# Feature-major matmuls of a two-layer transformer kernel: high weight tiles against 512 joined token columns, low tiles in a second pass

## What is computed

```python
def swiglu(x, w_gate, w_up, w_down):            # first network, two per layer
    return (jax.nn.silu(x @ w_gate) * (x @ w_up)) @ w_down      # 1024 -> 2816 -> 1024
...
z = u @ w_in[l]                                 # one wide projection per mixer
c_q, c_kv, k_rope, dq, dk, dv, p_in, z_gate = jnp.split(z, split_idx, axis=-1)
...
jnp.square(jax.nn.relu(x @ w1)) @ w2            # second network's feed-forward, 1024 -> 4096 -> 1024
```

## Time and profile before

| what | value |
|---|---|
| median of three executions | 2109.79 us (2108.17 to 2111.42) |
| profiled execution, its own time | 2109.59 us |
| span in the profile, first to last instruction | 2107.8 us |
| mean granted TensorE clock | 0.998 of full speed |
| TensorE matmul busy | 2079.7 us |
| VectorE busy | 1260.8 us |
| ScalarE busy | 1038.2 us |
| moved by DMA | 375.44 MB, mean 178 GB/s |

### The profile page before, as it was taken

One profiled execution on the slowest core, in us unless ns is written; L12 is line 12 of the kernel. 1 busy time (PEld: TensorE's weight loads), 2 busy tenths in 40 slices (PEclk: granted clock), 3 DMA queues, 4 the chain that ended last, 5 costly groups with the idle time before them and its releaser, 6 DMA issues.

```text
span 2107.8 us, 29081 instructions
## 1 busy us (share of the span) xinstructions
PE 2079.7 (99%) x12472; PEld 1843.5 (87%) x12472; DVE 1260.8 (60%) x1399; ACT 1038.2 (49%) x1327; POOL 89.7 (4%) x123
## 2 busy tenths in 40 slices
PE   7999999999999999999999999999999999999998
PEld 6999978889989898888898989888899888888897
DVE  5455586664455455676654565656755666567555
ACT  5444476454344344675443356643544466444442
POOL 1000100000000001000000000010100000100000
PEclk9999999999999999999999999999999999999999
DMA  8555444465566555444565564544755545455562
GB/s 297 181 190 181 156 159 140 140 210 181 189 193 211 182 185 191 147 143 140 169 218 183 176 221 134 176 152 153 243 183 193 192 154 180 150 175 196 188 192 80
DMA packets 178193, 375.44 MB, mean 178 GB/s; under 512 B 8480, under 2 KB 18848, under 8 KB 178064
## 3 DMA queue, kind: packets, MB, share of 16 engines
q1 hardware_dynamic: 174256, 360.67, 51.6%
q0 software_dynamic: 3808, 12.90, 2.0%
HBM read 372.49 MB, written 1.05 MB: 177 GB/s over the span
## 4 chain that ended last, share of the span: by engine, by line
PE 94%; DVE 3%; DMA 1%; ACT 1%; issue 0%; SPq 0%; POOLq 0%; POOL 0%; DVEq 0%
PE pb L1426 55%; PE pb L1443 32%; PE pb L1453 2%; DMA raw<-in_ffn_w_up_dram 1%; DVE lS L1978 1%; PE pb L1498 1%; DVE st L1984 1%; DVE st L1983 0%; DVE wl L1842 0%; PE pb L1506 0%; PE pb L1507 0%; PE pb L1551 0%; PE pb L1505 0%; DVE lS L1997 0%; DVE st L1986 0%
## 5 line engine op out<-in xcount | busy, mean ns | idle before, releaser
L1842 DVE TENSOR_TENSOR wl<-raw,wh 128x2048 fp32r<-128x2048 f32 (+3 forms) x348 | 780.6, 2249 | 282.3 <-ACT wh L1647 282.0
L1647 ACT ACTIVATE wh<-raw 128x2048 fp32r<-128x2048 f32 (+3 forms) x348 | 655.0, 1883 | 493.4 <-PE pb L1426 250.2
L1443 PE MATMUL pb<-xh,wl 128*128 128x256 f32 x1856 | 528.6, 285 | 0.0
L1443 PE MATMUL pb<-xl,wh 128*128 128x256 f32 x1856 | 525.2, 283 | 0.0
L1443 PE MATMUL pb<-xh,wh 128*128 128x256 f32 x1856 | 525.1, 283 | 0.0
L1426 PE MATMUL pb<-wl,xh 128*128 128x512 f32 x928 | 373.3, 402 | 2.5 <-DVE xl L1861 2.5
L1426 PE MATMUL pb<-wh,xl 128*128 128x512 f32 x928 | 362.2, 390 | 0.0
L1426 PE MATMUL pb<-wh,xh 128*128 128x512 f32 x928 | 361.7, 390 | 0.0
L1443 PEld LDWEIGHTS pb<-xh,wl 128*128 128x128 f32 x1856 | 356.1, 192 | 1.4 <-issue 0.7
L1443 PEld LDWEIGHTS pb<-xh,wh 128*128 128x128 f32 x1856 | 356.1, 192 | 0.8
L1443 PEld LDWEIGHTS pb<-xl,wh 128*128 128x128 f32 x1856 | 356.0, 192 | 0.0
(11 more groups left out here) (344 smaller groups left out, 1687.9 us busy)
## 6 DMA issues: line engine op xcount, KB each, us to landing
raw<-in_w_in_dram SPq DMA_DIRECT2D x100, 1024.0 KB, 5.2
raw<-in_w_ff_dram SPq DMA_DIRECT2D x64, 1024.0 KB, 5.3
raw<-in_ffn_w_up_dram SPq DMA_DIRECT2D x44, 1024.0 KB, 5.1
raw<-in_ffn_w_down_dram SPq DMA_DIRECT2D x44, 1024.0 KB, 4.9
raw<-in_ffn_w_gate_dram SPq DMA_DIRECT2D x42, 1024.0 KB, 5.2
raw<-in_w_branch_dram SPq DMA_DIRECT2D x24, 1024.0 KB, 5.0
raw<-in_w_out_dram SPq DMA_DIRECT2D x16, 1024.0 KB, 5.0
raw<-in_w_in_dram SPq DMA_DIRECT2D x4, 832.0 KB, 4.5
```

The lines of the kernel that those rows point to most:

```text
L1443: ins = e.matmul(o, w[:, n, c], x[:, it["kk"] + n, :], skip_group_check=True, start=(it["first"] and n == 0 and q == 0 and f % 2 == 0), st ...
L1647: e.activation(hi, raw, ACT.Copy).then_inc(m.high_done, 1)
L1842: e.tensor_tensor(lo, raw, hi.bitcast(F32), ALU.subtract).then_inc(m.low_done, 1)
```

## The change

All turned groups are replaced by `wide_group`. The high and low parts of x are put side by side in one buffer `x2`, so that one matmul moves 512 columns: 256 of the high part and 256 of the low part. For each feature tile, eight high weight tiles are multiplied with these 512 columns into a whole bank, and then eight low weight tiles with the 256 high columns into the first half of the bank. The second half of the bank holds (high weight)(low x), which has to be added to the first. ScalarE copies it to the destination (`"whalf"`, 256 columns) and VectorE adds the first half (256 columns), after which the bank is free. Silu, the product and the squared Relu are now applied to the sums in SBUF, 512 columns at a time, for two feature tiles. A weight unit is now eight tiles of 128 rows with 256 columns instead of four tiles with 512 columns; it has the same bytes. The q and k projections and the gate of the second mixer follow the same form. Bank pairs alternate between the banks 0 to 3 and 4 to 7 per 256 features.

```diff
@@ Memory.sbuf (line 145)
-        self.xh = A("xh", take(8192), [P, 8, S], F32R)
-        self.xl = A("xl", take(8192), [P, 8, S], F32R)
+        self.x2 = A("x2", take(16384), [P, 8, 2, S], F32R)
+        self.xh, self.xl = self.x2[:, :, 0, :], self.x2[:, :, 1, :]
@@ Plan (line 493): turned_group goes, wide_group comes
+    def wide_group(self, key, banks, epi):
+        j = self.take(key)
+        self.split(j)
+        need = self.need("X", range(8), [0, 1])
+        for i in range(2):
+            if i:
+                self.tick()
+            use = self.use(banks[i])
+            v = self.pe("wide", j=j, i=i, use=use, need=need)
+            epi(i, v["p"], use)
+        self.freed[j] = self.x_free = v["p"]
         self.tick()
@@ Plan.ffn1 (line 640)
-                    parts = [(0, 4), (4, 4)] if n == 512 else [(0, 8)]
-                    for b, name in ((0, gate), (1, up)):
-                        self.turned_group("X", [(name, (l,), k * P, kt, c0, n) for k, kt in parts],
-                                          self.pair(b, c0 > 512), self.silu_f if b == 0 else self.up_f(slot))
+                    for c in range(0, n, 256):
+                        side = (sum(chunks) + n0 - c0 - c) // 256 % 2 == 1
+                        q = c // 256
+                        self.wide_group((gate, (l,), 0, 8, c0 + c, 256), self.pair(0, side), self.gate_w(q))
+                        self.wide_group((up, (l,), 0, 8, c0 + c, 256), self.pair(1, side), self.up_w(q, slot + 2 * q))
@@ epilogues (lines 668 and 684): up_f and relu_f go
+    def gate_w(self, q):
+        def epi(i, p, use):
+            self.add("whalf", dst=("sg", q), i=i, p=p, use=use, n=self.next("half"), free=self.sg_free[q])
+            if i:
+                self.silu_n = self.next("silu")
+                self.add("wsilu", q=q, use=use, n=self.silu_n)
+        return epi
+    def up_w(self, q, slot):
+        def epi(i, p, use):
+            self.add("whalf", dst=("mn", q), i=i, p=p, use=use, n=self.next("half"), free=self.mn_free[q])
+            if i:
+                n = self.next("product")
+                self.add("wmul", q=q, use=use, s=self.silu_n, n=n)
+                self.sg_free[q] = ("product", n + 1)
+                self.mn_free[q] = self.split_into(slot, ("mn", q), ("product", n + 1))
+        return epi
+    def relu_w(self, q, slot):
...
+                self.add("wrelu", q=q, use=use, n=n, free=self.mn_free[q])
...
@@ Plan.ffn2 (line 729)
+            n_t = 0 if first else -2 * n_chunks % 4
...
+                for q in range(2):
+                    self.wide_group(("w_ff1_2", (l,), 0, 8, n0 + 512 * c + 256 * q, 256), self.pair(n_t % 2, n_t % 4 > 1),
+                                    self.relu_w(q, 4 * c + 2 * q))
+                    n_t += 1
@@ mixer1, mixer2: each turned_group with copy_f becomes copy_w; silu_g likewise takes two blocks
+    def copy_w(self, c0, dst, toks):
+        for q in range(2):
+            def epi(i, p, use, q=q):
+                self.add("whalf", dst=(dst, q), i=i, p=p, use=use, n=self.next("half"), free=None)
+                toks.append(("evac", use))
+            self.wide_group((self.W, (self.l,), 0, 8, c0 + 256 * q, 256), self.pair(q), epi)
@@ TensorE program (line 1430): "features" goes
+        elif k == "wide":
+            hi, lo = m.weights(it["j"])
+            bank, c = pb[use[0]], slice(i * P, i * P + P)
+            pe.wait_ge(m.low_done, it["j"] + 1)
+            pe.all_ready(it["need"])
+            pe.wait_ge(m.evac[use[0]], use[1])
+            for s in range(8):
+                e.matmul(bank[:, :], hi[:, s, c], m.x2[:, s, :, :].rearrange("p a s -> p (a s)"), start=(s == 0),
+                         stop=False, skip_group_check=True)
+            for s in range(8):
+                ins = e.matmul(bank[:, 0:S], lo[:, s, c], m.xh[:, s, :], start=False, stop=(s == 7),
+                               skip_group_check=True)
             ins.then_inc(m.pe_done, 1)
@@ ScalarE program (line 1656)
+        elif k == "whalf":
+            a.pe(p)
+            a.ready(it["free"])
+            e.activation(m.half(it["dst"], i), bank[:, S:2 * S], ACT.Copy).then_inc(m.half_copied, 1)
+        elif k == "wsilu":
+            q = it["q"]
+            a.emptied(use)
+            e.activation(m.sg[q][:, :], m.sg[q][:, :], ACT.Silu).then_inc(m.silu_done, 1)
@@ ScalarE program (line 1784), gsilu
-            a.pe(p)
-            e.activation(m.pair_of(("ggT", i)), bank[:, :], ACT.Tanh, scale=0.5).then_inc(m.gate_half, 1)
+            q = it["q"]
+            a.emptied(use)
+            e.activation(m.GT[0][:, 512 * q:512 * q + 512], m.pair_of(("ggT", q)), ACT.Tanh,
+                         scale=0.5).then_inc(m.gate_half, 1)
@@ VectorE program (line 1852)
+        elif k == "whalf":
+            o = m.half(it["dst"], i)
+            v.wait_ge(m.half_copied, n + 1)
+            e.tensor_tensor(o, bank[:, 0:S], o, ALU.add).then_inc(m.evac[use[0]], 1)
+        elif k == "wmul":
+            q = it["q"]
+            v.emptied(use)
+            v.wait_ge(m.silu_done, it["s"] + 1)
+            e.tensor_tensor(m.mn[q][:, :], m.mn[q][:, :], m.sg[q][:, :], ALU.mult).then_inc(m.product, 1)
+        elif k == "wrelu":
+            q = it["q"]
+            v.emptied(use)
+            v.ready(it["free"])
+            e.scalar_tensor_tensor(m.mn[q][:, :], m.sg[q][:, :], 0.0, m.sg[q][:, :], ALU.max,
+                                   ALU.mult).then_inc(m.product, 1)
```

More of the change, by code:

```diff
@@ L682, in relu2 @@
         self.sg_free[i] = ("evac", use)
-    def relu_f(self, slot):
+    def relu_w(self, q, slot):
         def epi(i, p, use):
-            self.relu2(i, p, use)
-            self.mn_free[i] = self.split_into(slot + 2 * i, ("mn", i), ("evac", use))
+            self.add("whalf", dst=("sg", q), i=i, p=p, use=use, n=self.next("half"), free=self.sg_free[q])
+            if i:
+                n = self.next("product")
+                self.add("wrelu", q=q, use=use, n=n, free=self.mn_free[q])
+                self.sg_free[q] = ("product", n + 1)
+                self.mn_free[q] = self.split_into(slot, ("mn", q), ("product", n + 1))
         return epi
@@ L964, in mixer1 @@
         qk = []
-        self.turned_group("X", [(W, (l,), 512 * i, 4, 416, 512) for i in range(2)], self.pair(0), self.copy_f("dqT", qk),
-                          by_bank=False)
-        self.turned_group("X", [(W, (l,), 512 * i, 4, 928, 512) for i in range(2)], self.pair(1), self.copy_f("dkT", qk),
-                          by_bank=False)
+        self.copy_w(416, "dqT", qk)
+        self.copy_w(928, "dkT", qk)
         self.dqk = list(qk)
@@ L1133, in mixer2 @@
         self.group(self.cols(W, l, 2576, 0, gelu(0, "zv", zv)) + self.cols(W, l, 2064, 1, gelu(1, "zu", zu)))
-        wide = lambda c0: [(W, (l,), 512 * i, 4, c0, 512) for i in range(2)]
         def decay():
@@ L1146, in mixer2 @@
         self.decayed, lr = [], []
[L1147 to L1148 removed]
+        self.copy_w(0, "gqT", gq)
+        self.copy_w(512, "gkT", gk)
         j = self.take((W, (l,), 0, 8, 2048, 16))
@@ L1158, in mixer2, with silu_g @@
         self.gq, self.gk, self.gv = gq, gk, gv
-        def silu_g(i, p, use):
-            n = self.next("gate_half")
-            self.add("gsilu", i=i, p=p, use=use, n=n)
-            gg.append(("evac", use))
-        self.turned_group("X", wide(1536), self.pair(1), silu_g, by_bank=False)
+        for q in range(2):
+            def silu_g(i, p, use, q=q):
+                self.add("whalf", dst=("ggT", q), i=i, p=p, use=use, n=self.next("half"), free=None)
+                if i:
+                    n = self.next("gate_half")
+                    self.add("gsilu", q=q, use=use, n=n)
+                    gg.append(("gg_ready", n + 1))
+                    self.g_free[0] = ("gg_ready", n + 1)
+            self.wide_group((W, (l,), 0, 8, 1536 + 256 * q, 256), self.pair(1 - q), silu_g)
         while not self.decayed:
@@ L2064, in dve_program @@
         elif k == "gsilu":
-            o = m.pair_of(("ggT", i))
+            q = it["q"]
+            o = m.pair_of(("ggT", q))
             v.wait_ge(m.gate_half, n + 1)
-            e.scalar_tensor_tensor(o, o, 1.0, bank[:, :], ALU.add, ALU.mult).then_inc(m.evac[use[0]], 1)
+            e.scalar_tensor_tensor(o, m.GT[0][:, 512 * q:512 * q + 512], 1.0, o, ALU.add,
+                                   ALU.mult).then_inc(m.gg_ready, 1)
         elif k == "gdecay":
```

50 lines of the change are left out of this document (14 added, 36 removed).

## The result

The changed kernel takes 2114.24 us, the median of 20 executions (2111.91 to 2116.31). The kernel before, timed beside it, takes 2110.60 us (20 executions, 2108.14 to 2113.91). The ratio is 1.0016, with an interval of 1.0009 to 1.0022. That is within 0.2% of no change, on the slower side, where 2096.7 us and a range up to 2107 us had been forecast.

What follows compares the result with a forecast made beforehand. The prediction took TensorE's matmul stream to bound the kernel: 2109.6 us - 24.3 (saving) + 3 x 1.4 + 5.4 (waits in second halves of `ffn1`) + 1.8 (waits in `ffn2`) = 2096.7 us, range 2084 to 2107.

Steps and rivals of the forecast that it cites:

- What bounds the kernel: Whole kernel: TensorE has work for 99% of the span and is 94% of the chain, so a shorter matmul stream shows.
- The saving, 13.1 ns per tile: Wide matmuls on TensorE: one instruction fewer for each of 1856 weight tiles, 24.3 us saved.
- The rival that the saving is absent: Wide matmuls: the 13.1 ns do not belong to an instruction, a 512-column matmul costs 240 ns; result 2121 us, chance 0.05.
- The gap rule of the Trainium skill: Matmul price N/2.4 + 2.5 ns: a tile would save 2.5 ns, the change 4.6 us; prediction went by trace rows instead.
- The loop, 6.29 and 6.44 us: ScalarE and VectorE wait for each other once per gate or up unit, taking these times against TensorE's 5.55 us.
- Second halves of `ffn1`, 3 x 1.4 + 5.4: Down projections after ten wide units: TensorE waits 1.4 us three times, 5.4 us in the first, which has table steps.
- `ffn2` part one, 2 x 0.9: Down projection after two wide units, twice: TensorE waits 0.9 us each for a bank, 1.8 in all (0 to 2.6).
- "Mixers: I take 0", bound 4: Copy and add for q, k and gate in four mixers: no wait expected, at most 1 us each, 0 to 4.
- "Cost 0, covered by this lead": Weight loads with 1 KB instead of 2 KB runs: no cost, since loads are issued over 22 us before use.
- The rival "slower": ScalarE and VectorE: loop much longer; 0.4 us more per unit makes waits 31 us, result 2117 us; chance 0.05.
- The rival "between these": TensorE waits of 20 to 28 us, result 2105 to 2114 us, no change that can be told; chance 0.08.
- The rival without lag: ScalarE's and VectorE's lag never reaches TensorE: waits 0 to 4 us, result 2085 to 2089, centre 2087; chance 0.22.

Runs made afterwards that it cites:

- experiments 2 and 8: Experiment 2 has its own line; 8 is that kernel with each 512-column matmul split back into two of 256: 2111.73 us against 2093.59 us.
- experiment 2: Changed kernel with Silu, product and its splits, squaring and gate's Tanh appended one tick later, behind the next unit's high split on ScalarE: 2093.59 us.
- experiment 5: Changed kernel with the bank pairs of the two gate blocks in the second mixer exchanged, so the next item doesn't need the bank just filled: 2105.72 us.
- experiment 4: Kernel before with only the weight units of the change (8 tiles by 256 columns, 1 KB runs); matmuls and epilogues as before: 2111.63 us, ratio 1.0003.
- experiment 9: Changed kernel with both the later epilogues of experiment 2 and the exchanged gate banks of experiment 5: 2090.62 us, ratio 0.9904 to the kernel before.
- experiment 3: Changed kernel with the table steps started at tick 28 instead of 40, ahead of the first ten-unit stretch: 2109.43 us, ratio 0.9998 to the kernel before.
- experiment 6: Changed kernel with high and low weight tiles alternating (512 columns, 256, 512, ...) instead of eight and eight: 2116.38 us, ratio 1.0031 to the kernel before.
- experiment 7: Changed kernel with the eight low tiles ahead of the eight high tiles in each item: 2113.21 us, ratio 1.0015 to the kernel before.

## Why the prediction was wrong

Measured 2114.2 against predicted 2096.7: 17.5 us to account for.

- *What bounds the kernel: right.* A shorter stream shows once nothing else waits: 18.1 us by experiments 2 and 8, of the 20.3 that the spacing of the matmuls gives.
- *The saving, 13.1 ns per tile: wrong in size.* Ten units, 160 tiles, gained 57.59 - 55.84 = 1.75 us, 10.9 ns per tile. For 1856 tiles that is 20.3 us: 4.0 us short of the 24.3; by experiments 2 and 8 it is 18.1, 6.2 short. The rows of 226.9 and 120.0 ns come from long pieces of one width; a high pass after a low one takes 0.02 to 0.03 us longer. The rival that the saving is absent was wrong. The gap rule of the Trainium skill (TensorE: Matmul & The Clock Gate, Back-to-back issue gap), which is given there for a single matmul and comes to 2.5 ns per tile, does not fit the 9.8 to 10.9 ns measured in this stream either.
- *The loop, 6.29 and 6.44 us: right* (6.33 and 6.45). The add of 256 columns took 0.42 us, as assumed.
- *Second halves of `ffn1`, 3 x 1.4 + 5.4: right*, 10.0 us in four waits, the longest 5.4. The wait comes from the order of two queues, which experiment 2 shows by taking it away.
- *`ffn2` part one, 2 x 0.9: right*, 2 x 0.8.
- *"Mixers: I take 0", bound 4: wrong, the largest miss.* Two waits of 2.6 us, and 1.9 for the clock behind one: 7.1 us, and 8 to 8.5 by experiment 5. The step compared a need of 0.8 us with an item of 2.7. It left out that the gate has the same loop as `ffn1`, with the decay's steps and table loads in it besides, though the prediction named these two gates as the places where ScalarE waits for VectorE. A copy 4.6 us late, and a product that wants its bank after one item of 2.8 us, were not walked through.
- *"Cost 0, covered by this lead" for the DMA: wrong at the start*, where no lead has built up. 2.0 us more on `mn` and, at a clock of 0.54 for 8 matmuls (3.1 us instead of 1.8), about 1.5 us more: 3.5. The rows quoted for it were of a queue that wasn't full. Experiment 4, with the runs alone, has 1.4 of the 2.0 us of wait; the other 0.6 are open.
- *The clock after a wait: a term that was missing.* 1.9 us behind the 5.4 us wait and the two sums just named. The mean clock went from 0.998 to 0.995; 0.003 of 2110 us is 6.3, and the three places sum to 5.3.
- *Small:* `lS` +0.9.

Sum: 4.0 (saving) + 7.1 (gates with clock) + 3.5 (start) + 1.9 (clock) + 0.9 = 17.4 of the 17.5 us. With the saving by experiments 2 and 8 it is 2 us too much. The medians can't settle that, and I leave the saving at 18 to 20 us. The waits and the clock are read from one profiled execution (2114.5 us), so each term holds for that one.

The rival "slower" had the sign, not the mechanism: the loop wasn't longer. The rival "between these", waits of 20 to 28 us and 2105 to 2114 us, comes nearest by the number, for new waits and clock came to 24.9 us (10.0 + 1.5 + 7.1 + 3.5 + 1.9 + 0.9). That is luck: it named no gate, no DMA and no clock. The rival without lag (2087) is what experiment 9 comes near (2090.6), once the order is mended. The range failed because the bounds of the mixers and of the DMA were left out of its upper end, and because it had no term for what a wait sets off in the clock.

## What to carry to other kernels

When an epilogue is spread over two in-order engines, write down both queues in the changed order, for every place where it is used, and look for a step that waits for the other engine with the next unit's preparation behind it; appending that step after the preparation was worth 20.6 us here. A lag that is hidden in one place surfaces where the next item needs the bank just filled, so follow such places one by one. Price layouts where the queue is full, not where it is idle, and give each new wait of some us a second term for the clock behind it, with 0 as its lower end.

## What the runs showed of the hardware

- A wait in a dense matmul stream can cost more than its length. Behind the wait of 5.4 us in the changed kernel the granted clock was 0.50 up to 194 us, and 60 matmuls of 512 columns took 15.5 us instead of 13.6; behind one of the two waits of 2.6 us it was 0.57 over 4 us. It was 0.57 behind a wait of 2.3 us in experiment 3, too. Behind the waits of 1.5 us, behind the other one of 2.6 us and behind one of 1.7 us in experiment 2 it stayed at 1.00.
- The length of a wait does not settle what the clock does: at the start it was 0.50 behind a wait of 1.9 us in experiment 9 and 1.00 behind one of 2.3 us in experiment 6 (45 to 48 us in both). Nor is the price fixed: behind the same wait of 5.5 us the 60 matmuls took 15.5 us in experiment 5 and 16.8 in experiment 7.
- A pass of eight 512-column matmuls takes 1.84 us behind a pass of 256 columns and 1.81 behind 512, whichever pass is first in the item.
- In a full queue, runs of 1 KB moved at some 350 GB/s and runs of 2 KB at some 385 at best; where the queue isn't full, a unit of 1 MB took 5.4 and 5.3 us.
